# Splitting the row gathers of the value stage into an up half and a down half

## Chip, cores and metric

The kernel runs on one core of one Trainium2 chip. The metric is the device time of one execution in microseconds (us). The core has five engines that run side by side, each with its own program in order: TensorE (PE, with its weight loads PEld), VectorE (DVE), ScalarE (ACT), GpSimd (POOL) and SyncE (SP). They wait for each other through semaphores. 16 DMA engines move the data; SP, ACT and POOL issue transfers to them, each on a queue of its own.

## What is computed

One layer of a decoder trunk, 512 tokens of width 2048, all in float32: attention and a gated unit, then a product-key expert layer (PEER), then a gate. The change touches the expert layer alone:

```python
N_EXPERTS, PEER_HEADS, PEER_TOPK = 128 * 128, 8, 16

def peer(a, w_q, k1, k2, u_exp, v_exp):
    # experts, gates: for each token and head the 16 best of 16384, and their weights
    ...
    u_sel = jnp.take(u_exp, e_c, axis=0)              # rows of the first matrix
    h = jnp.einsum('bthkd,btd->bthk', u_sel, a_c)     # one dot product per pick
    w = (g_c * jax.nn.gelu(h)).astype(a_c.dtype)
    v_sel = jnp.take(v_exp, e_c, axis=0)              # rows of the second matrix
    return jnp.einsum('bthk,bthkd->btd', w, v_sel)    # weighted sum of the rows
```

Each expert is a row of 2048 numbers (8 KB) in each of the two matrices. A token has 8 x 16 = 128 picks.

## The kernel before, in words

The expert layer is done in two ways. For the first 352 tokens (`TD`) it is dense: all 16384 experts are multiplied through TensorE and gated by a table in device memory that is zero where a token did not pick an expert. For the other 160 tokens (128 in the last tile, 32 more spread as 4 sets over the partitions) rows are gathered, one expert for each of 128 partitions at a time: a **pick**. There are 160 picks (`PICKS`), 0 to 127 for the last tile, 128 to 159 for the 32 tokens.

The dense part has two stages. In the **key stage** each step takes 128 experts of the first matrix. In the **value stage** there are 16 groups of 8 **beats**; a beat takes a tile of 1 MB of the second matrix from `s_pv`, and makes 48 matmuls of 352 columns. Float32 is split in two parts for TensorE, so each beat needs from ScalarE the high half of its weights (`wH`, line 603), and from VectorE the low half (`lo`, `wL`, line 1025), which TensorE waits for. `wH` and `wL` have two buffers each; `raw`, the tile as it was loaded, has four in this stage.

The activations of a group are made one group ahead. For each beat SP loads a tile `pre_in` and a tile of gates `gate_in` (lines 415 and 416), POOL multiplies them (`apply_gates`, line 566), ScalarE writes the high half (`actH`, line 859) and VectorE the low half (`weight_lo`, `actL`, line 1555). SP loads the next pair of tiles when the low half two beats back is written.

A pick is done in these steps. POOL gathers 128 rows of `uv_rows`, a table with the two matrices side by side, into a buffer `rows` of 16 KB a partition (`gather`, line 558). VectorE multiplies the first half by the tokens' activations and sums up (`dot`, line 1529). ScalarE puts the sum through gelu and the gate's weight (lines 876 and 880). VectorE adds the second half times that weight to `hT`, or to `b_acc` for the 32 tokens (`add_row`, lines 1538 and 1543), and counts up `pick_done`. That frees the buffer.

The order is written out by hand. `u_step` and `v_step` say which steps of which picks fall into which beat. The first 64 picks (`U_PICKS`) go with the key stage and share three buffers; 60 of them are gathered there while POOL also scatters gates into device memory (line 539). Picks 64 to 159 go with the value stage and take turns in two buffers, `rows3` and `rows4`; `dot` and `add_row` of them lie one or two to a beat over beats 2 to 119. In a beat VectorE does the first of its pick steps, then `lo`, then its other pick steps, then `weight_lo`:

```python
for o in steps[0:1]:
    pick_step(o)
v_low(g, q)
for o in steps[1:]:
    pick_step(o)
v_end(g, q, g % 2, m, 0)
```

POOL does in each beat the multiply of `apply_gates`, and behind it the gathers of that beat; pick j + 2 is gathered behind the add of pick j.

Of the kernel before, what the change touches and what calls it, by code (L numbers as in the profile page):

```python
# [51 lines left out]
U_PICKS, LATE = 64, 4  # L52
# [16 lines left out]
ROW_AT, ROW_USED, ROW_TURN = [], [], []  # L69
# [83 lines left out]
def trunk_layer(nc, a, stream, out, gates_dram, pre_dram):  # L153
# [8 lines left out]
    def at(name, shape, dt, offset):  # L162
        return nc.alloc_sbuf_tensor_at(name, [P] + shape, dt, offset=base + offset)
# [40 lines left out]
    rows = [at(f"rows{i}", [2, D], F, o) for i, o in enumerate((W0, W0 + 16 * KB, W0 + 32 * KB, A0, A0 + 16 * KB))]  # L204
# [70 lines left out]
    with ctx:  # L275
        ps = ctx.enter_context(nc.psum_tensor("ps", [P, 8, 512], F))

        def sem(name):
            return ctx.enter_context(nc.semaphore(name))
# [41 lines left out]
        gain_row_loaded, tok_done_h, tok_copied, a_tok_ready = (  # L321
            sem("gain_row_loaded"), sem("tok_done_h"), sem("tok_copied"), sem("a_tok_ready"))
        row_landed = [sem(f"row_landed{i}") for i in range(5)]
        dot_done, dot_gelu, pick_weighed, pick_done = sem("dot_done"), sem("dot_gelu"), sem("pick_weighed"), sem("pick_done")
        b_loaded, rep_ready, b_tok_done, b_tok_early, b_tok_ready = (
            sem("b_loaded"), sem("rep_ready"), sem("b_tok_done"), sem("b_tok_early"), sem("b_tok_ready"))
# [146 lines left out]
        def _(pool):  # L473
# [75 lines left out]
            def gather(j):  # L549

                if j == U_PICKS:
                    pool.wait_ge(b_tok_ready, 1)
                if j == A_PICKS:
                    pool.wait_ge(b_loaded, 32 * SETS)
                if ROW_USED[j] >= 0:
                    pool.wait_ge(pick_done, ROW_USED[j] + 1)
                ids = idx_s[:, j:j + 1] if j < A_PICKS else idx_b[:, j - A_PICKS:j - A_PICKS + 1]
                pool.indirect_dma_start(  # L558
                    out=rows[ROW_AT[j]][:, :, :].rearrange("p a d -> p (a d)"), out_offset=None, in_=a["uv_rows"],
                    in_offset=bass.IndirectOffsetOnAxis(ap=ids, axis=0)).then_inc(row_landed[ROW_AT[j]], 16)  # L560
# [7 lines left out]
            for j in range(U_PICKS - LATE + 1):  # L568
                gather(j)
                if j >= 1:  # L570
                    for n in range(added, min(added + 4, HEADS * NTD * TOPK)):
                        add_gates(n)
                        added = n + 1
            assert added == HEADS * NTD * TOPK
            for c in range(GROUP):
                apply_gates(c, c % 2)
                if c % 2 == 0 and U_PICKS - LATE + 1 + c // 2 < U_PICKS:
                    gather(U_PICKS - LATE + 1 + c // 2)
            for j in range(U_PICKS, U_PICKS + 2):
                gather(j)  # L580
# [432 lines left out]
        def _(dve):  # L1013
# [517 lines left out]
            def add_row(j):  # L1531

                dve.wait_ge(pick_weighed, j + 1)
                if j >= 1:
                    dve.wait_ge(pick_done, j)
                v3 = rows[ROW_AT[j]][:, 1, :].rearrange("p (a b) -> p a b", a=KD)
                if j < A_PICKS:
                    V.scalar_tensor_tensor(hT[:, :, TA:T], v3, pick_w[:, j:j + 1], hT[:, :, TA:T],  # L1538
                                           ALU.mult, ALU.add).then_inc(pick_done, 1)
                elif j == A_PICKS:  # L1540
                    V.tensor_scalar(b_acc[:, :, :], v3, pick_wb[:, 0:1], None, ALU.mult).then_inc(pick_done, 1)
                else:
                    V.scalar_tensor_tensor(b_acc[:, :, :], v3, pick_wb[:, j - A_PICKS:j - A_PICKS + 1], b_acc[:, :, :],  # L1543
                                           ALU.mult, ALU.add).then_inc(pick_done, 1)

            def pick_step(o):

                if o % 2 == 0:
                    dot(o // 2)
                else:  # L1550
                    add_row(o // 2)
# [640 lines left out]
```

## Time and profile before

| | |
|---|---|
| median of 3 runs | 3055.32 us (3047.83 to 3064.97) |
| profiled execution, its own time | 3049.59 us |
| its span (first to last instruction) | 3047.9 us |
| TensorE busy (matmuls) | 2972.5 us, 98% of the span |
| VectorE busy | 2208.6 us, 72% |
| ScalarE busy | 1252.3 us, 41% |
| POOL busy | 1223.3 us, 40% |
| moved by the DMA engines | 798.00 MB, 262 GB/s on average |

Shares are means over the whole program, in which the stages have different limits. The value stage runs from about 1782 to 2829 us of the span, the gathers from 1064 to 2742 us. Matmuls are pipelined: one is listed with 0.32 us while the next starts 0.16 us behind it. A line such as "PE ps L1720 <- DVE wL L1025: 36.0, 30, 2.9" reads: TensorE stood idle before the matmul of line 1720, until VectorE had written `wL` in line 1025, for 36.0 us in all, 30 times, at most 2.9 us.

### The profile page before, as it was taken

The numbers are of one execution on the slowest core, as the hardware profiler recorded it, in microseconds if no ns is written. First come the engines' busy times: TensorE is split into PE (matmuls) and PEld (weight loads), VectorE is DVE, ScalarE is ACT, GpSimd is POOL, SyncE is SP. The second block draws the span as 40 slices with busy tenths as digits, with TensorE's granted clock in tenths as the row PEclk, the third lists the DMA queues.
The fourth block names the chain that finished last, engine by engine and source line by source line (L and its number), as shares of the span: only waits on it lengthen the run. The fifth ranks groups of instructions, "written<-read, shape, count | busy, mean of one in ns | idle before, by whom it ended". The sixth has DMA issues, their size and how long they took to land.

```text
span 3047.9 us, 43192 instructions
## 1 busy us (share of the span) xinstructions
PE 2972.5 (98%) x16888; PEld 2784.3 (91%) x16888; DVE 2208.6 (72%) x2801; ACT 1252.3 (41%) x1818; POOL 1223.3 (40%) x717
## 2 busy tenths in 40 slices
PE   9999999999999999999999999999999999999998
PEld 7888678899999999999999999999999999999887
DVE  5466754579788777777777678878877888886545
ACT  5224542333332433333333334555555545555422
POOL 1010000018888888888887123233323244540000
PEclk9999999999999999999999999999999999999999
DMA  8462222235545599999999799999999999994222
GB/s 294 164 238 83 70 97 96 83 125 137 133 127 139 131 379 339 360 356 359 357 344 372 299 359 370 397 376 389 393 396 384 383 374 385 370 360 164 97 96 97
DMA packets 191348, 798.00 MB, mean 262 GB/s; under 512 B 66672, under 2 KB 119936, under 8 KB 127200
## 3 DMA queue, kind: packets, MB, share of 16 engines
q1 hardware_dynamic: 90768, 405.36, 36.3%
q0 software_dynamic: 81616, 367.62, 33.2%
q10 hardware_dynamic: 18816, 23.11, 2.2%
q8 instruction: 85, 1.39, 0.2%
q14 instruction: 63, 0.52, 0.0%
HBM read 745.46 MB, written 50.51 MB: 261 GB/s over the span
## 4 chain that ended last, share of the span: by engine, by line
PE 33%; POOL 24%; DMA 21%; DVE 12%; issue 7%; ACT 2%; SPq 0%; ACTq 0%; DVEq 0%; POOLq 0%
POOL gates L539 22%; PE ps L1720 10%; PE ps L1721 10%; PE ps L1722 10%; DMA rows<-uv_rows,idx_s 9%; DMA gate_in<-gates 6%; DMA rows<-uv_rows,idx_b 4%; DVE wL L1025 4%; DVE rows L1529 2%; DVE hT L1538 2%; POOL rows L558 2%; DMA gates<-gates_r,idx_d 1%; DVE b_acc L1543 1%; POOL pre_in L566 1%; ACT wH L603 1%
## 5 line engine op out<-in xcount | busy, mean ns | idle before, releaser
L1720 PE MATMUL ps<-aH,wH 128*128 128x352 f32 (+2 forms) x3088 | 1063.0, 344 | 8.1 <-DVE wL L1025 8.1
L1721 PE MATMUL ps<-aL,wH 128*128 128x352 f32 (+2 forms) x3088 | 1059.3, 343 | 0.0
L1722 PE MATMUL ps<-aH,wL 128*128 128x352 f32 (+2 forms) x3088 | 1059.0, 343 | 0.0
L1025 DVE TENSOR_TENSOR wL<-raw,wH 128x2048 fp32r<-128x2048 f32 x333 | 778.7, 2338 | 195.6 <-ACT wH L603 194.4
L539 POOL DMA_INDIRECT gates<-gates_r,idx_d x384 | 754.1, 1964 | 381.8 <-DVE gates_r L1440 244.5
L603 ACT ACTIVATE wH<-raw 128x2048 fp32r<-128x2048 f32 x333 | 636.5, 1911 | 657.4 <-PE ps L1722 630.3
L1720 PE MATMUL ps<-actH,wH 128*128 128x352 f32 x2048 | 669.1, 327 | 37.0 <-DVE wL L1025 36.8
L1721 PE MATMUL ps<-actL,wH 128*128 128x352 f32 x2048 | 665.4, 325 | 0.0
L1722 PE MATMUL ps<-actH,wL 128*128 128x352 f32 x2048 | 665.0, 325 | 0.0
L1720 PEld LDWEIGHTS ps<-aH,wH 128*128 128x128 f32 x3088 | 581.0, 188 | 49.9 <-DVE wL L1025 8.4
L1721 PEld LDWEIGHTS ps<-aL,wH 128*128 128x128 f32 x3088 | 581.0, 188 | 38.4 <-issue 0.7
L1722 PEld LDWEIGHTS ps<-aH,wL 128*128 128x128 f32 x3088 | 581.0, 188 | 38.3
L1720 PEld LDWEIGHTS ps<-actH,wH 128*128 128x128 f32 x2048 | 388.5, 190 | 47.1 <-DVE wL L1025 46.8
L1722 PEld LDWEIGHTS ps<-actH,wL 128*128 128x128 f32 x2048 | 388.9, 190 | 0.0
L1721 PEld LDWEIGHTS ps<-actL,wH 128*128 128x128 f32 x2048 | 388.8, 190 | 0.0
L1529 DVE SCALAR_TENSOR_TENSOR rows<-rows,ps 128x2048 f32<-128x2048 f32 x128 | 292.2, 2283 | 122.8 <-DMA rows<-uv_rows,idx_s 122.4
L566 POOL TENSOR_TENSOR pre_in<-pre_in,gate_in 128x352 f32<-128x352 f32 x128 | 183.2, 1432 | 336.0 <-DMA gate_in<-gates 335.5
L558 POOL DMA_INDIRECT rows<-uv_rows,idx_s x128 | 188.2, 1470 | 321.2 <-DVE hT L1538 287.9
L1538 DVE SCALAR_TENSOR_TENSOR hT<-rows,pick_w,hT 128x2048 f32<-128x2048 f32 x128 | 301.4, 2355 | 0.6 <-ACT pick_w L880 0.5
L1449 DVE TENSOR_TENSOR ut<-ps,rstd 128x352 f32<-128x352 f32 x128 | 67.0, 524 | 148.1 <-PE ps L1722 139.9
L876 ACT ACTIVATE dots<-dots 128x1 f32<-128x1 f32 x128 | 26.0, 203 | 358.9 <-DVE rows L1529 356.6
L1555 DVE TENSOR_TENSOR actL<-pre_in,actH 128x352 fp32r<-128x352 f32 x128 | 74.9, 585 | 50.0 <-ACT actH L859 50.0
(270 smaller groups left out, 2251.2 us busy)
## 6 DMA issues: line engine op xcount, KB each, us to landing
raw<-s_pu SPq DMA_DIRECT2D x128, 1024.0 KB
raw<-s_pv SPq DMA_DIRECT2D x128, 1024.0 KB, 7.1
gates<-zeros POOLq DMA_DIRECT2D x22, 1024.0 KB, 8.5
pre<-ut ACTq DMA_DIRECT2D x128, 176.0 KB
pre_in<-pre SPq DMA_DIRECT2D x128, 176.0 KB, 7.6
gate_in<-gates SPq DMA_DIRECT2D x128, 176.0 KB, 8.9
raw<-s_out SPq DMA_DIRECT2D x16, 1024.0 KB
raw<-s_pq SPq DMA_DIRECT2D x16, 1024.0 KB
```

The costliest lines, as they stand in the source:

```text
L539: pool.indirect_dma_start(out=gates_flat, out_offset=bass.IndirectOffsetOnAxis(ap=idx_d[0:m, t, c:c + 1], axis=0), in_=gates_r[0:m, t, c:c ...
L558: pool.indirect_dma_start(out=rows[ROW_AT[j]][:, :, :].rearrange("p a d -> p (a d)"), out_offset=None, in_=a["uv_rows"], in_offset=bass.In ...
L566: nc.gpsimd.tensor_tensor(pre_in[b][:, :], pre_in[b][:, :], gate_in[b][:, :], ALU.mult).then_inc(act_gated, 1)
L603: A(wH[parity][:, :], raw[at_n][:, :], ACT.Copy).then_inc(hi_ready, 1)
L1025: V.tensor_tensor(wL[parity][:, :], src[:, :], wH[parity][:, :].bitcast(F), ALU.subtract).then_inc(lo_ready, 1)
L1449: V.tensor_tensor(ut[b][:, :], ps[:, 6 + b, 0:TD], rstd[:, 0:TD], ALU.mult).then_inc(chunk_scaled, 1)
L1529: V.scalar_tensor_tensor(r3, r3, 1.0, act_of, ALU.mult, ALU.mult, accum_out=d).then_inc(dot_done, 1)
L1538: V.scalar_tensor_tensor(hT[:, :, TA:T], v3, pick_w[:, j:j + 1], hT[:, :, TA:T], ALU.mult, ALU.add).then_inc(pick_done, 1)
L1555: V.tensor_tensor(actL[b][:, j, 0:TD], src[:, :], actH[b][:, j, 0:TD].bitcast(F), ALU.subtract).then_inc(act_wlo, 1)
L1720: mm(out, wh, xh, start=start, stop=False, skip_group_check=skip_group_check)
L1721: mm(out, wh, xl, start=False, stop=False, skip_group_check=skip_group_check)
L1722: return mm(out, wl, xh, start=False, stop=stop, skip_group_check=skip_group_check)
```

## The change

For picks 64 to 159 `gather` issues two indirect DMAs instead of one: the first brings 128 rows of 8 KB of the first matrix into the first half of the buffer, the second the rows of the second matrix into the other half. They come from two new tables, `u_rows` and `v_rows`; `uv_rows` stays for picks 0 to 63. The first half counts up the semaphore that the joint row had, the second one of two new semaphores, for which `add_row` waits. `dot` waits as before.

```diff
+        v_row_landed = [sem(f"v_row_landed{i}") for i in range(2)]
...
                 ids = idx_s[:, j:j + 1] if j < A_PICKS else idx_b[:, j - A_PICKS:j - A_PICKS + 1]
+                if j >= U_PICKS:
+                    for half, landed, table in ((0, row_landed[ROW_AT[j]], a["u_rows"]), (1, v_row_landed[ROW_AT[j] - 3], a["v_rows"])):
+                        pool.indirect_dma_start(
+                            out=rows[ROW_AT[j]][:, half, :], out_offset=None, in_=table,
+                            in_offset=bass.IndirectOffsetOnAxis(ap=ids, axis=0)).then_inc(landed, 16)
+                    return
                 pool.indirect_dma_start(
                     out=rows[ROW_AT[j]][:, :, :].rearrange("p a d -> p (a d)"), out_offset=None, in_=a["uv_rows"],
...
                 dve.wait_ge(pick_weighed, j + 1)
+                if j >= U_PICKS:
+                    dve.wait_ge(v_row_landed[ROW_AT[j] - 3], 16 * ROW_TURN[j])
...
+        "u_rows": v["peer_u"][0],
+        "v_rows": v["peer_v"][0],
```

On POOL, at the first beats of the value stage that gather, the program before has this order; `rows_89` and `rows_90` are the two buffers, and the words in brackets are the semaphores that a row waits for:

```order
L558 DMA rows_89<-uv_rows,idx_s 128x4096 [waits pick_done]
L566 TENSOR_TENSOR pre_in_134<-pre_in_134,gate_in_136 128x352 [waits gates_loaded0,pre_loaded0]
L558 DMA rows_90<-uv_rows,idx_s 128x4096 [waits pick_done]
L566 TENSOR_TENSOR pre_in_135<-pre_in_135,gate_in_137 128x352 [waits gates_loaded1,pre_loaded1]
L558 DMA rows_89<-uv_rows,idx_s 128x4096 [waits pick_done]
```

The same place with the change (its lines lie some lower, so 566 is 573):

```order
L561 DMA rows_89<-u_rows,idx_s 128x2048 [waits pick_done]
L561 DMA rows_89<-v_rows,idx_s 128x2048
L573 TENSOR_TENSOR pre_in_134<-pre_in_134,gate_in_136 128x352 [waits gates_loaded0,pre_loaded0]
L561 DMA rows_90<-u_rows,idx_s 128x2048 [waits pick_done]
L561 DMA rows_90<-v_rows,idx_s 128x2048
L573 TENSOR_TENSOR pre_in_135<-pre_in_135,gate_in_137 128x352 [waits gates_loaded1,pre_loaded1]
L561 DMA rows_89<-u_rows,idx_s 128x2048 [waits pick_done]
L561 DMA rows_89<-v_rows,idx_s 128x2048
```

Nothing changed its place; a second gather without a wait of its own stands between each gather and the multiply behind it.

On VectorE, in the middle of the value stage, with the change:

```order
L1547 SCALAR_TENSOR_TENSOR hT<-rows_89,pick_w,hT 128x16x128 [waits pick_done,v_row_landed0,pick_weighed]
L1032 TENSOR_TENSOR wL_73<-raw_69,wH_71 128x2048 [waits hi_ready]
L1536 SCALAR_TENSOR_TENSOR rows_90,dots<-rows_90,ps 128x2048 [waits row_landed4]
L1564 TENSOR_TENSOR actL_85<-pre_in_135,actH_83 128x352 [waits act_whi]
L1547 SCALAR_TENSOR_TENSOR hT<-rows_90,pick_w,hT 128x16x128 [waits pick_done,v_row_landed1,pick_weighed]
L1032 TENSOR_TENSOR wL_74<-raw_70,wH_72 128x2048 [waits hi_ready]
```

The instructions and their order are those of before (lines 1538, 1025, 1529 and 1555 there); only the waits for `v_row_landed` are new, and a `lo` stands behind each such add.

## Rows read from the trace of the kernel before

**Rows 1.** Windows: busy time, matmuls (x), mean clock, DMA share; key stage twice, value stage.
```profile
core 0: us, PE busy (x) PEld busy (x) DVE busy (x) ACT busy (x) POOL busy (x), PEclk, DMA share, GB/s
1150.00:1350.00 200.00, 200.00 (x1252) 200.00 (x1251) 155.46 (x110) 69.52 (x91) 168.88 (x94) 1.00 0.99 350
1350.00:1550.00 200.00, 198.74 (x1243) 198.45 (x1242) 155.87 (x109) 68.00 (x91) 165.58 (x94) 1.00 1.01 357
...
1782.50:2829.40 1046.90, 1009.91 (x6194) 999.63 (x6192) 835.98 (x593) 543.51 (x923) 346.00 (x216) 0.99 0.92 363
```
**Rows 2.** Waits from 1790 to 2735 us: total us, times, longest.
```profile
DVE rows L1529 <- DMA rows<-uv_rows,idx_s: 96.6, 45, 4.5
...
PEld ps L1720 <- DVE wL L1025: 45.7, 33, 3.2
...
PE ps L1720 <- DVE wL L1025: 36.0, 30, 2.9
DVE rows L1529 <- DMA rows<-uv_rows,idx_b: 35.3, 18, 3.4
```
**Rows 3.** Timeline of VectorE: start, duration, instruction, idle time before it and releaser.
```profile
2340.01 2.29 DVE L1529 SCALAR_TENSOR_TENSOR rows<-rows,ps 128x2048 f32<-128x2048 f32 x1 [3.18 <-DMA rows<-uv_rows,idx_s]
...
2343.29 0.53 DVE L1555 TENSOR_TENSOR actL<-pre_in,actH 128x352 fp32r<-128x352 f32 x1 [0.99 <-ACT actH L859]
2343.73 2.35 DVE L1538 SCALAR_TENSOR_TENSOR hT<-rows,pick_w,hT 128x2048 f32<-128x2048 f32 x1
2345.99 2.28 DVE L1025 TENSOR_TENSOR wL<-raw,wH 128x2048 fp32r<-128x2048 f32 x1
...
2360.36 2.29 DVE L1529 SCALAR_TENSOR_TENSOR rows<-rows,ps 128x2048 f32<-128x2048 f32 x1 [4.54 <-DMA rows<-uv_rows,idx_s]
...
2362.57 2.28 DVE L1025 TENSOR_TENSOR wL<-raw,wH 128x2048 fp32r<-128x2048 f32 x1
```
**Rows 4.** Timeline of TensorE, the matmul behind the first of these chains.
```profile
2348.33 0.42 PE L1720 MATMUL ps<-actH,wH 128*128 128x352 f32 x1 [1.63 <-DVE wL L1025]
```
**Rows 5.** Windows of 3.5 us, behind a long stall and behind a short one.
```profile
2003.50:2007.00 3.50, 3.50 (x16) 3.50 (x15) 3.30 (x3) 2.83 (x6) 1.31 (x2) 0.56 0.88 274
...
2349.00:2352.50 3.50, 3.50 (x24) 3.50 (x23) 3.50 (x3) 2.62 (x7) 1.09 (x2) 1.00 0.90 299
```
**Rows 6.** The gathers of line 558 from 1780 to 2760 us.
```profile
DMA to landing us min/median/max: 9.8/11.7/15.8
```
**Rows 7.** Chain of waits from 1790 to 2735 us, shares by line.
```profile
by line: DMA rows<-uv_rows,idx_s 27.9%; DMA gate_in<-gates 17.9%; DMA rows<-uv_rows,idx_b 12.2%; DVE wL L1025 9.1%; DVE rows L1529 7.3%; DVE hT L1538 7.1%; issue 7.1%; POOL pre_in L566 3.2%; DVE b_acc L1543 2.9%; DVE actL L1555 1.4%; ACT ac
```
**Rows 8.** Window of the value stage's body.
```profile
1790.00:2735.00 945.00, 908.82 (x5561) 899.01 (x5560) 767.72 (x526) 491.45 (x854) 335.20 (x210) 0.99 0.97 383
```
**Rows 9.** The page's DMA parts: a queue's packets, MB and share; an issue's KB and landing.
```profile
q1 hardware_dynamic: 90768, 405.36, 36.3%
q0 software_dynamic: 81616, 367.62, 33.2%
...
raw<-s_pv SPq DMA_DIRECT2D x128, 1024.0 KB, 7.1
```
**Rows 10.** Timeline of POOL, two gathers one behind the other.
```profile
1063.64 1.01 POOL L558 DMA_INDIRECT rows<-uv_rows,idx_s  x1 [0.30 <-issue]
1064.95 0.98 POOL L558 DMA_INDIRECT rows<-uv_rows,idx_s  x1 [0.30 <-issue]
```
**Rows 11.** Timeline of POOL, a gather beside the `lo` of 2345.99.
```profile
2346.35 2.78 POOL L558 DMA_INDIRECT rows<-uv_rows,idx_s  x1 [4.63 <-DVE hT L1538]
```
**Rows 12.** Multiplies of line 566 from 1790 to 2735 us, and waits there.
```profile
L566 POOL TENSOR_TENSOR pre_in<-pre_in,gate_in x117: 942/956/3059, 1789.9 to 2728.3; 128x352 f32<-128x352 f32 x117
...
POOL pre_in L566 <- DMA gate_in<-gates: 315.1, 103, 8.8
...
DVE actL L1555 <- ACT actH L859: 42.8, 38, 4.0
```
**Rows 13.** Timelines of VectorE and POOL: a `lo` behind a multiply that was still waiting.
```profile
2441.79 3.03 DVE L1025 TENSOR_TENSOR wL<-raw,wH 128x2048 fp32r<-128x2048 f32 x1
...
2440.38 2.29 POOL L566 TENSOR_TENSOR pre_in<-pre_in,gate_in 128x352 f32<-128x352 f32 x1 [0.90 <-DMA gate_in<-gates]
```

## Prediction, before the change was run

> **What bounds the kernel now.** I read the windows by stage first, then the waits of the value stage, then single beats. In the key stage, while the same kind of gathers runs, TensorE is busy for 200.00 us of 200 and then for 198.74 of 200 [rows 1]. In the value stage the first and the last matmul lie 1046.9 us apart, for 128 beats of 48 matmuls (6144), so 8.18 us a beat. The key stage made 1252 matmuls in 200 us, which is 7.67 us for 48. At that pace the value stage would take 982 us, so about 65 us of it is lost; 50 of the 6194 matmuls in that window are not the beats' own and take some 8 us, which leaves 57 us.
>
> The waits say what is late [rows 2]: TensorE stands for 36.0 us (30 times) before a matmul, its weight load for 45.7 us (33 times), both for VectorE's low half of the weights, `lo`. VectorE itself stands for a gathered row, 96.6 and 35.3 us, 63 times. Single beats join the two. In one, the dot of a pick waits 3.18 us for its row, then come the low half of an activation, the add of the pick and `lo`, and TensorE gets its weights 1.63 us late, at 2348.33 [rows 3, 4]. In the other shape the dot waits 4.54 us and `lo` follows it at once. Of the stalls from 1850 to 2735 that are longer than half a microsecond there are 25, and all have such a dot less than 10 us ahead, 12 in the first shape, 13 in the second. A long stall costs more than itself: behind the stall at 2003, a stretch of 3.5 us has a mean clock of 0.56 where a beat with a short stall has 1.00 [rows 5]. That is the lower of the two levels, 1.2 GHz instead of 2.4, for nearly all of it. Five such stretches stand in this stage's body (from 1874, 2003, 2522, 2587 and 2720), so some 5 x 1.7 = 8.5 us.
>
> So the bound of this stage is a loop through two row buffers: pick j is added, POOL gathers pick j+2 into the same buffer, the row lands 11.7 us (median; 9.8 to 15.8) behind its issue [rows 6], the dot may start. TensorE pays for its late turns. The chain of waits of this stage says the same: 27.9 and 12.2% of it are rows on their way, 17.9% the gates' tiles [rows 7].
>
> **What the change does, step by step.** It touches picks 64 to 159 alone, the ones of the value stage.
>
> 1. *The dot waits for half the bytes.* The first half should land sooner by what the other half took on the queue. At the stage's 383 GB/s [rows 8] the 1 MB that no longer lies ahead is 2.7 us. The nearest row for a transfer of 1 MB is that of the weights, 7.1 us to landing [rows 9], and 11.7 - 7.1 = 4.6 us. Nothing at all is the lower bound, if the engines' queues are so full that order decides. I take 2.7, the careful end of the two measured prices. The row waits are 131.9 / 63 = 2.1 us each and at most 4.5, so with 2.7 us most are gone.
>
> 2. *The add has a new wait.* The second half is issued behind the first. Two gathers one behind the other took POOL 1.01 and 0.98 us with 0.30 us between them [rows 10]; but a gather issued while a `lo` runs on VectorE takes 2.78 us [rows 3, 11]. So the second half is issued 1.3 to 3.1 us later than the joint row was, and lands at 11.7 + 1.3 = 13.0 to 14.8 us. (The Trainium skill, SBUF — State Buffer, Who interferes with whom, infers that a tensor_tensor does not hold up descriptor generation. By that only the 1.3 would stand. The trace has 2.78 us beside a `lo`, which is one, so it speaks against it.) The dot starts at 9.0 and ends at 11.3. In the first shape the add started 3.7 us behind the dot's start [rows 3], which would be 12.7. So there the second half is the later by 0.3 to 2.1 us, and the chain is 0.6 to 2.4 us earlier than before (15.4), not 2.7. In the second shape nothing stands between dot and `lo`, so it gains all 2.7. Of the mean of the two views of the stall, (36.0 + 45.7) / 2 = 41 us, I keep 5 us for the first shape: 36 us go. With them go the low clocks, 8 us. Gross: 44 us.
>
> 3. *The loop still closes.* From issue to landing of the second half at most 14.8 us, add 2.35 us: 17.2 us, and the buffer has 2 x 945 / 93 = 20 us between its turns (93 picks in 945 us). This is why I don't expect the new wait to become the bound.
>
> 4. *POOL issues 96 gathers more*, 1.3 to 3.1 us each, 125 to 298 us. It was busy for 346 of 1046.9 us [rows 1], so there is room in sum. Behind each pair stands a gating multiply, of which the body of the stage has 117; they waited for their own data 315.1 us in 103 turns, 3.1 us each [rows 12]. That wait hides one more gather, whether it meets `lo` or not. The other 14 have no such cover: 14 x 1.3 = 18 us at least come later. Behind them wait ScalarE's high half and VectorE's low half of the activations, which are used by TensorE a whole group of eight beats later; they reach TensorE only where VectorE stands for them ahead of the next `lo`. It stood for them 42.8 us in 38 turns, mostly the 0.98 us in which ScalarE first weighs the pick [rows 3, 12]. I price this at 3 us, with 0 and 18 as ends.
>
> 5. *The transfers.* Bytes are the same, packets are smaller. SP's queue, mostly packets of 8 KB, moved 405.36 MB in 36.3% of the engines' time; POOL's queue, mostly 16 KB rows, 367.62 MB in 33.2% [rows 9]. Per MB that is equal within 1%. So splitting costs nothing on the engines themselves. But they have little left: 0.97 busy over the body of this stage [rows 8], and 0.99 and 1.01 in the two stretches of the key stage in which TensorE was hardly stopped [rows 1]. If all of the stage's transfers must be squeezed into less time, the share rises with it. From 0.97 to 0.99 that allows 2.0% of 945 us, 19 us; to 1.01, 4.0%, 37 us. The middle is 28 us, less than the 44 of step 2, so **this is the end that I take**.
>
> The Trainium skill has two rules on this (DMA: Bandwidth & Descriptors). Its section Measured and the one on the anatomy of a DMA give about 2.0 us fixed for each DMA plus bytes / 436 GB/s: by that the first half lands 2.4 us sooner, and step 2 would keep some 1 us per stall more. Its section Where 436 GB/s comes from names some 358 GB/s as what HBM gives a core when both cores of a pair stream and 435 as the fabric's ceiling. The trace has 383 GB/s with this core alone, so the lower figure doesn't bind here; by the higher one some 13% would be left, and step 5 would cap nothing.
>
> 6. *The waits themselves:* VectorE gets 96 semaphore waits more on instructions that it issues anyway, with 945 - 768 = 177 us idle in this stretch [rows 8]; nothing.
>
> **The sum.** 28 us by the transfers' limit, less 3 us of POOL: 25 us. Against the profiled execution (3049.59 us, span 3047.9) that gives 3024.6. The median of the runs shown is 5.7 us above that execution, so for the median I say 3055.3 - 25 = 3030 us. A difference of 0.5%, 15 us, is about what a measurement of this kernel can tell from none.
>
> **Rivals.**
> - *The DMA engines are full already* (0.97 is their end; the queues' order only decides who waits). Then the half that comes early is paid by the other half, by the gates or by the next row: in the first shape the add stands where the dot stood, and the chain to `lo` ends when it did. For it: bits of idle in the engines come only when both row buffers are taken. Against it: 1.01 in the key stage. Gain 0 to 14 us, 3041 to 3055. Here belongs the case in which the change doesn't do what it says, because the first half of pick j+2 queues behind the second half of pick j+1. By the rule of 358 GB/s this would be the outcome too; that sentence changes no number. Chance 0.30.
> - *POOL becomes late* (the other sign). A pair of gathers holds POOL up to 5.8 us where both meet a `lo`. The multiply behind it then starts while VectorE is in a long instruction, and the next `lo` is stretched: 3.03 us with a multiply that was still waiting, against 2.28 [rows 3, 13]. If each of the 96 further gathers pushes a multiply into this, it costs 96 x 0.75 = 72 us of VectorE. VectorE has a fifth of its time free, so I count half, 36 us, on the way to TensorE; with the 18 us of step 4 that is 54 us against the 28 gained: 26 us slower, 3081. It decides from the point where the multiplies without a wait for their data are a majority. Against it: POOL's wait of 3.1 us on average. Milder forms end at 3071. Chance 0.14.
> - *The forecast's own spread*: all 44 us go (3011) or 16 only (3039). Chance 0.56.
>
> So: faster by over 0.5% 0.56, within it 0.30, slower 0.14. The range reaches from 3002 (all of the 57 us of the stage's loss but a few) to 3062, which takes in the no-change case with the spread of its runs (3047.83 to 3064.97) and leaves most of the slower one out.
>
> **What would show it.** Waits of the dot for rows well under half of 131.9 us; a new wait of the add for the second table, a few tens of us; TensorE's wait for `lo` below 15 us and fewer low clocks; the body at a DMA share of 0.99 or more, over 390 GB/s; POOL's gathers 96 more at 1.0 or 2.8 us, its wait for the gates' data smaller. I am wrong if the dot's wait shrinks and TensorE's doesn't (then the add or the gates took its place), if the share stays at 0.97 with the same pace, or if `lo` at 3.0 us becomes common.

## The result, and the profile after

The changed kernel takes 3004.12 us (median, 3000.28 to 3008.28), the kernel before, measured beside it, 3051.57 us (3045.14 to 3064.97): 47 us less, ratio 0.985 (95% interval 0.9823 to 0.9878). A second measurement gave 2999.9 us against 3053.32, ratio 0.9829 (0.9814 to 0.9844). The forecast had the sign and the mechanism, and only half of the size: 25 us, with 3030 as the time. Its range, 3002 to 3062, just takes in the first of the two medians and not the second. One of the six executions of e8b below took 7626.78 us at a mean TensorE clock of 0.488; it counts in that run's median (3001.35 without it) and not in its ratio.

The windows of the profile after, in the columns of [rows 1]:

```profile
1150.00:1350.00 200.00, 196.24 (x1219) 195.07 (x1218) 153.97 (x108) 67.84 (x90) 168.98 (x90) 1.00 0.99 341
1350.00:1550.00 200.00, 194.98 (x1208) 193.53 (x1207) 150.15 (x106) 66.47 (x86) 165.06 (x93) 1.00 0.99 348
...
1790.00:2690.00 900.00, 895.88 (x5579) 893.35 (x5578) 783.01 (x528) 495.58 (x854) 485.60 (x303) 1.00 1.00 402
```

The last row answers to [rows 8]: TensorE is busy for 896 of 900 us, the mean clock is 1.00 where it was 0.99, and the DMA engines move 402 GB/s instead of 383. From its first to its last matmul the value stage takes 996.9 us:

```profile
1790.30:2787.20 996.90, 992.78 (x6195) 990.15 (x6193) 852.19 (x593) 546.11 (x923) 506.64 (x312) 1.00 0.95 382
```

It was 1046.9 [rows 1], so 50 us went there, more than the span lost in all (3047.9 to 3006.1, 42 us). The difference lies in the key stage: in this execution the value stage begins 8 us later. Its program is the one of before; a later section comes back to it.

The waits from 1790 to 2690 us after, columns as in [rows 2]:

```profile
POOL pre_in L573 <- DMA gate_in<-gates: 234.8, 80, 9.1
ACT actH L866 <- POOL pre_in L573: 135.7, 67, 6.0
...
DVE actL L1564 <- ACT actH L866: 75.1, 59, 6.5
...
DVE rows L1536 <- DMA rows<-u_rows,idx_b: 12.6, 12, 2.8
DVE rows L1536 <- DMA rows<-u_rows,idx_s: 10.2, 18, 1.4
PEld ps L1729 <- DVE wL L1032: 6.7, 9, 1.5
PE ps L1729 <- DVE wL L1032: 3.9, 6, 1.2
...
DVE b_acc L1552 <- DMA rows<-v_rows,idx_b: 0.9, 1, 0.9
```

The dot's wait for its row fell from 131.9 us [rows 2] to 22.8. TensorE's wait for `lo` fell from 36.0 to 3.9 us, that of the weight load from 45.7 to 6.7. The new wait, of the add for the second table, came up once, for 0.9 us. What grew stands behind POOL: ScalarE waited 135.7 us for the gating multiply, and VectorE 75.1 us for ScalarE's half, 42.8 before [rows 12]. In the kernel before, from 1790 to 2735 us, the first of these two was:

```profile
ACT actH L859 <- POOL pre_in L566: 18.8, 21, 5.6
```

What the two cost TensorE can be no more than its few us of waits that are left.

The landings of the two gathers, from the page's view of the DMA issues (median from issue to landing):

```profile
raw<-s_pv SPq DMA_DIRECT2D x128, 1024.0 KB, 9.2
...
rows<-u_rows,idx_s POOLq DMA_INDIRECT x64, 9.1
rows<-v_rows,idx_s POOLq DMA_INDIRECT x64, 10.6
```

The joint row took 11.7 us [rows 6], the first half now takes 9.1: 2.6 us sooner. The second half takes 10.6 from its own issue, which lies 1.3 us behind the first one where nothing holds it up. The weights' tile lands at 9.2 instead of 7.1 us [rows 9]; it has slack, ScalarE waited for it once, for 0.9 us.

### The profile page after: what moved, and what is told of

It is laid out like the page before. It is cut to its first block and busy times, and to the rows that moved or that the text cites. A ratio compares the mean times of both kernels' runs of the same rounds, so it can differ in the third digit from the quotient of the medians.

```text
span 3006.1 us, 43288 instructions
## 1 busy us (share of the span) xinstructions
PE 2958.6 (98%) x16888; PEld 2775.7 (92%) x16888; DVE 2226.4 (74%) x2801; ACT 1254.9 (42%) x1818; POOL 1390.1 (46%) x813
## 5 line engine op out<-in xcount | busy, mean ns | idle before, releaser
L1729 PE MATMUL ps<-aH,wH 128*128 128x352 f32 (+2 forms) x3088 | 1063.5, 344 | 12.8 <-DVE wL L1032 12.7
L540 POOL DMA_INDIRECT gates<-gates_r,idx_d x384 | 766.0, 1995 | 384.3 <-DVE gates_r L1447 244.6
L1729 PE MATMUL ps<-actH,wH 128*128 128x352 f32 x2048 | 661.7, 323 | 4.1 <-DVE wL L1032 3.9
L573 POOL TENSOR_TENSOR pre_in<-pre_in,gate_in 128x352 f32<-128x352 f32 x128 | 235.3, 1839 | 251.7 <-DMA gate_in<-gates 250.3
L1536 DVE SCALAR_TENSOR_TENSOR rows<-rows,ps 128x2048 f32<-128x2048 f32 x128 | 292.1, 2282 | 61.3 <-DMA rows<-uv_rows,idx_s 50.7
L1547 DVE SCALAR_TENSOR_TENSOR hT<-rows,pick_w,hT 128x2048 f32<-128x2048 f32 x128 | 320.9, 2507 | 1.2 <-ACT pick_w L887 1.0
L561 POOL DMA_INDIRECT rows<-u_rows,idx_s x64 | 105.3, 1645 | 116.3 <-DVE hT L1547 99.0
```

What stands on the lines that cost most here:

```text
L540: pool.indirect_dma_start(out=gates_flat, out_offset=bass.IndirectOffsetOnAxis(ap=idx_d[0:m, t, c:c + 1], axis=0), in_=gates_r[0:m, t, c:c ...
L561: pool.indirect_dma_start(out=rows[ROW_AT[j]][:, half, :], out_offset=None, in_=table, in_offset=bass.IndirectOffsetOnAxis(ap=ids, axis=0) ...
L573: nc.gpsimd.tensor_tensor(pre_in[b][:, :], pre_in[b][:, :], gate_in[b][:, :], ALU.mult).then_inc(act_gated, 1)
L1536: V.scalar_tensor_tensor(r3, r3, 1.0, act_of, ALU.mult, ALU.mult, accum_out=d).then_inc(dot_done, 1)
L1729: mm(out, wh, xh, start=start, stop=False, skip_group_check=skip_group_check)
```

## The experiments

Theory A was that the time came from the dot's earlier start. The rivals: B, that it was the smaller packets and how they share the engines with SP's queue; C, that the DMA engines, as in my step 5, set the end; D, that POOL sets it. Each ratio is to the kernel before, measured beside the run.

**e1: the dot waits for both halves.** Packets, tables and the further gathers stay.

```diff
                 dve.wait_ge(row_landed[ROW_AT[j]], 16 * ROW_TURN[j])
+                if j >= U_PICKS:
+                    dve.wait_ge(v_row_landed[ROW_AT[j] - 3], 16 * ROW_TURN[j])
```

Expected:

> The change with one wait more: the dot of picks 64 to 159 waits for the second half too. Packets, tables, POOL's 96 further gathers stay. Theory A (the gain is the dot's earlier start): the gain goes, and a little more since the second half is issued 1.3 to 3.1 us later than the joint row was: 3045 to 3080 us, VectorE waits for the second table 130 us or more, TensorE for the low half of the weights 36 us or more. Rival B (the gain is the packets of 8 KB, which share the engines more evenly with SP's queue): 3000 to 3015 us, few waits.

Measured: 3079.6 us, ratio 1.007 (1.0047 to 1.0093) to the kernel before, which was at 3052.96 here. Its waits from 1790 to 2690 us:

```profile
DVE rows L1538 <- DMA rows<-v_rows,idx_s: 106.8, 43, 5.9
...
PEld ps L1731 <- DVE wL L1032: 62.0, 38, 5.1
...
PE ps L1731 <- DVE wL L1032: 50.9, 32, 4.8
DVE actL L1566 <- ACT actH L866: 42.3, 36, 6.5
DVE rows L1538 <- DMA rows<-v_rows,idx_b: 37.5, 12, 5.9
```

The row waits are back, at 144 us and up to 5.9 us long. The whole gain is gone, and 27 us more. Behind a pair's first issue the second half lands 12.6 us later (median over this trace's pairs), where the joint row took 11.7: somebody now waits for the later of two. B falls as the source of the gain, since the packets of 8 KB are all there.

**e2: the second matrix's rows first.**

```diff
-                    for half, landed, table in ((0, row_landed[ROW_AT[j]], a["u_rows"]), (1, v_row_landed[ROW_AT[j] - 3], a["v_rows"])):
+                    for half, landed, table in ((1, v_row_landed[ROW_AT[j] - 3], a["v_rows"]), (0, row_landed[ROW_AT[j]], a["u_rows"])):
```

Expected:

> The change with the two gathers of a pick in the other order, the second matrix's rows first; the dot waits for the gather issued last. Theory A: like e1_dot_waits_both, 3045 to 3080 us. Rival B: 3000 to 3015 us.

Measured: 3076.96 us, ratio 1.0069 (1.0049 to 1.0089). So the order in which a pair is issued decides between 1.5% faster and 0.7% slower. Semaphores, tables and the number of instructions are the same in both.

**e4: no rows of the second matrix.** 94 of the second gathers are left out, and the add takes what lies in the buffer.

```diff
+                        if half == 1 and j >= U_PICKS + 2:
+                            continue
...
-                    dve.wait_ge(v_row_landed[ROW_AT[j] - 3], 16 * ROW_TURN[j])
+                    dve.wait_ge(v_row_landed[ROW_AT[j] - 3], 16)
```

Expected:

> The change without the second matrix's rows for picks 66 to 159: 94 gathers of 1 MB, a quarter of the value stage's bytes, are left out, and the add takes what lies in the buffer. Theory A (after the change the DMA engines are full but TensorE isn't kept from work by them): 2995 to 3005 us, within 10 us of the change, DMA share near 0.78. Rival C (the DMA engines at a share of 1.00 hold the stage back now): the rest of TensorE's waits in the value stage goes, 2985 us or less.

Measured: 2997.28 us, ratio 0.9815 (0.9794 to 0.9835). The windows of its value stage:

```profile
1777.00:2766.60 989.60, 989.07 (x6194) 988.15 (x6192) 822.92 (x593) 544.12 (x923) 341.65 (x218) 1.00 0.79 285
```

With a quarter of the bytes and all of POOL's further gathers away, the stage takes 989.6 us instead of 996.9, with TensorE busy for 989.07 of them. So some 7 us is what transfers, POOL and late rows together cost the changed kernel in this stage (one execution each; in the change's second profile the stage took 999.4 us). C falls for the changed kernel: its share of 1.00 is not what holds it.

**e5: one more tile a beat**, into memory that this stage doesn't use.

```diff
                 sp.dma_start(gate_in[b][:, :], gates_rows[:, c, :]).then_inc(gates_loaded[b], 16)
+                if isinstance(c, int) and c >= 2 * GROUP:
+                    for _ in range(1):
+                        if extra_count[b]:
+                            sp.wait_ge(extra_landed[b], 16 * extra_count[b])
+                        sp.dma_start(ut[b][:, :], pre_dram[c, :, :]).then_inc(extra_landed[b], 16)
+                        extra_count[b] += 1
```

Expected:

> The change plus one further load of 176 KB from the stored tiles into unused memory in each of 112 beats of the value stage: 5.6% more bytes there, which nobody computes with. Rival C, my step 5 (a DMA share of 1.01 is the end): the body would need 1.055 and is stretched by 4% or more: 3040 us or more. Theory A (the share does not show the end, packets of 0.309 us for 8 KB leave room up to 424 GB/s, the body is at 402): little, 3004 to 3020 us.

Measured: 3031.88 us, ratio 0.9948 (0.9932 to 0.9964): between the two, so neither expectation held. The window of its body:

```profile
1790.00:2690.00 900.00, 875.70 (x5415) 869.92 (x5414) 758.36 (x513) 481.59 (x832) 461.72 (x297) 1.00 1.02 413
```

5.6% more bytes made the rate rise to 413 GB/s, not to the 424 that would have kept the pace. The edge is near, but beyond what the change needs. SP's queue didn't wait for the further loads in this window, so it is not the edit's own wait that delays the rest.

**e9: a wider one**, 10% more bytes; the same edit with another source and a target of 640 columns.

```diff
+    extra_in = [at(f"extra_in{i}", [640], F, C0 + 7 * KB + 2560 * i) for i in range(2)]
...
+                        sp.dma_start(extra_in[b][:, :], stream["pv"][c, :, 0:640]).then_inc(extra_landed[b], 16)
```

Expected:

> e5_one_more_tile with a wider load, 320 KB instead of 176 KB, so 10% more bytes in 112 beats. If 413 GB/s is the engines' end, as that run suggests: a beat moves 402 GB/s x 7.79 us = 3.13 MB with the change, 3.46 MB here, 8.37 us at 413 GB/s; times 112 beats, 0.58 us more each: 65 us over the change, 3065 to 3075 us, GB/s near 413. If the stage is held by how late each row is and not by the bytes: the rate rises beyond 413 and the time stays below 3050 us.

Measured: 3078.33 us, ratio 1.008 (1.0063 to 1.0096), 78 us above the change's second measurement (2999.9), beside which it ran.

```profile
1790.00:2690.00 900.00, 851.36 (x5166) 842.64 (x5165) 724.79 (x491) 458.63 (x794) 433.42 (x282) 0.98 1.02 410
```

More demand gave no more rate: 410 GB/s after 413. The time is 3 us above the 3065 to 3075 that 413 gave; with the measured 410 in the same sum a beat takes 3.46 MB / 410 GB/s = 8.44 us, which is 73 us. So the mean rate of this stage's mixture ends at 410 to 413 GB/s, with a share of 1.02. Single slices of 22.5 us reach 419 in e5 and 421 in e9, and 424 already in the body of the kernel before, beside others of 349: its own profile had stretches well above its mean.

**e6: POOL gets three small memsets behind each pair.**

```diff
+                    for i in range(3 if j >= U_PICKS + 2 else 0):
+                        if j > U_PICKS + 2 or i:
+                            pool.wait_ge(filled, 3 * (j - U_PICKS - 2) + i)
+                        nc.gpsimd.memset(ut[0][:, :], 0.0).then_inc(filled, 1)
```

Expected:

> The change plus three small memsets on POOL behind each pair of gathers of picks 66 to 159, as a dearer pair would be (some 1 us a pick, read from its trace). If POOL has the room that its 46% of busy time says: 3000 to 3010 us. If POOL is near its end, since ScalarE now waits for its multiply 135.7 us where it was 18.8: 3015 us or more, with stretched instructions of VectorE.

Measured: 3002.09 us, ratio 0.9848 (0.9823 to 0.9873). POOL is busy for 573 of 900 us instead of 486, and the time stays:

```profile
1790.00:2690.00 900.00, 896.76 (x5579) 894.13 (x5578) 785.62 (x530) 496.50 (x860) 572.99 (x580) 1.00 1.00 402
```

**e7: all 160 picks split**, those of the key stage too.

```diff
-                if j >= U_PICKS:
-                    for half, landed, table in ((0, row_landed[ROW_AT[j]], a["u_rows"]), (1, v_row_landed[ROW_AT[j] - 3], a["v_rows"])):
+                if True:
+                    for half, landed, table in ((0, row_landed[ROW_AT[j]], a["u_rows"]), (1, v_row_landed[ROW_AT[j]], a["v_rows"])):
...
-                if j >= U_PICKS:
-                    dve.wait_ge(v_row_landed[ROW_AT[j] - 3], 16 * ROW_TURN[j])
+                dve.wait_ge(v_row_landed[ROW_AT[j]], 16 * ROW_TURN[j])
```

Expected:

> The change for all 160 picks, the 64 of the key stage too. There POOL is busy 84% of the time with scattering gates, and gets 64 gathers more of 1.3 us: 83 us. Theory A: row waits of the key stage (25 to 50 us, of which TensorE feels 5 to 10) go, but POOL's later gates may be waited for: 2995 to 3015 us. Rival D (POOL is the bound of the key stage): the scatter ends some 80 us later and the value stage's first gates are late: 3030 us or more.

Measured: 3103.82 us, ratio 1.0179 (1.0154 to 1.0204), about 100 us above the change. One window of its key stage, its waits from 1060 to 1780 us, and POOL's timeline there:

```profile
1150.00:1350.00 200.00, 177.73 (x1052) 175.61 (x1051) 134.05 (x95) 58.84 (x78) 170.24 (x98) 0.96 0.92 307
```

```profile
DVE rows L1536 <- DMA rows<-u_rows,idx_s: 118.0, 37, 6.6
PEld ps L1728 <- DVE wL L1032: 74.2, 23, 6.1
PE ps L1728 <- DVE wL L1032: 67.5, 23, 5.8
```

```profile
1202.88 1.55 POOL L540 DMA_INDIRECT gates<-gates_r,idx_d  x1 [0.30 <-issue]
1204.74 1.36 POOL L561 DMA_INDIRECT rows<-u_rows,idx_s  x1 [0.30 <-issue]
1206.40 1.87 POOL L561 DMA_INDIRECT rows<-v_rows,idx_s  x1 [0.30 <-issue]
1208.58 1.61 POOL L540 DMA_INDIRECT gates<-gates_r,idx_d  x1 [0.30 <-issue]
```

Here POOL hardly ever waits for data: every instruction shown starts 0.30 us behind the last one, 170 of 200 us are busy, and 98 times 0.30 us is the rest. It was as full before (168.88 us busy with 94 instructions [rows 1]), so each further gather delays all that stands behind it. From 1060 to 1780 us the dots wait for rows 118 us, where they waited 25.9 in the kernel before and 50.7 in the change's first profile, and TensorE pays 67.5 us and runs at a mean clock of 0.96 in the window shown. The last scatter of gates ends at 1754.5 us instead of 1666.5, as D had it, but the loss is taken in the key stage itself: the value stage begins at 1878.1 us (1790.5 in the change) and then takes 1001.1 us. D is right for the key stage: the split that gains 1.5% in one stage loses more than twice that in the other.

**e8: the first half already behind the dot.** Pick j+2's first half is gathered when the dot of pick j is done, its second half behind the add as now.

```diff
-                if ROW_USED[j] >= 0:
+                if halves == (0,):
+                    pool.wait_ge(dot_done, ROW_USED[j] + 1)
+                elif ROW_USED[j] >= 0:
                     pool.wait_ge(pick_done, ROW_USED[j] + 1)
...
-                        if o % 2 == 1 and o // 2 + 2 < PICKS:
-                            gather(o // 2 + 2)
+                        if o // 2 + 2 < PICKS:
+                            gather(o // 2 + 2, (o % 2,))
```

Expected:

> The change, with the first half of pick j+2 gathered as soon as the dot of pick j is done, a step before its add; the second half behind the add as now. Theory A: the row waits left in the value stage (23 us) go, but TensorE waits only some 5 us there: 2998 to 3006 us, no difference to the change. Rival C: the engines are full and the earlier half delays the second half and the gates: 3005 to 3020 us.

Measured: 3001.02 us, ratio 0.9814 (0.9791 to 0.9836). The wait for the first half is practically gone (from 22.8 us to 0.8), TensorE's is 2.4 us:

```profile
PE ps L1733 <- DVE wL L1036: 2.4, 3, 1.6
...
DVE rows L1540 <- DMA rows<-u_rows,idx_s: 0.6, 3, 0.2
DVE rows L1540 <- DMA rows<-u_rows,idx_b: 0.2, 1, 0.2
```

**a1 and e8b: the change and this version again**, measured side by side.

> The change itself once more, beside e8b_up_half_after_dot on the same chip: 3000 to 3008 us. Its key stage, whose program is that of before, should wait for rows as before (some 25 us) if the 50 us in the first profile of the change were chance.

> The kernel of e8_up_half_after_dot once more, to settle whether it beats the change. Theory A: TensorE lost only 5 us in the value stage to waits with the change and 3 us in this one, so the two are within 0.15%, 4 us, and the intervals overlap. If the earlier half is worth more than the profile shows: 2995 us or less with the change at 3004.

Measured: 2999.9 us, ratio 0.9829 (0.9814 to 0.9844), and 3002.22 us, ratio 0.983 (0.9812 to 0.9847). No difference. What the earlier half removes is a wait that TensorE no longer felt. In a1 the key stage had few waits:

```profile
DVE rows L1536 <- DMA rows<-uv_rows,idx_s: 9.6, 6, 3.9
...
PE ps L1729 <- DVE wL L1032: 1.3, 1, 1.3
```

Those are its waits from 1060 to 1700 us. In the change's first profile the same two were 50.0 us and 8.7 us, in that of before 24.6 and 4.1. Across the profiled executions of all programs with this key stage, the dots' waits there range from 6.8 us (e8) to 50.0 and TensorE's from nothing to 8.7 (e8b had 20.4 and none). In the other runs that have the new tables and this key stage the value stage begins between 1777.0 and 1787.0 us, in the kernel before at 1782.5, in the change's first profile at 1790.5. So the 8 us by which it began late there vary from execution to execution and are no effect of the new tables. The variation's source was not looked for.

## Why the prediction was wrong in its size

**Step 1, the dot's lead: right.** I took 2.7 us and a landing at 9.0 us; measured were 2.6 and 9.1. The row waits fell to a sixth. The 2.4 us that I had worked out by the Trainium skill (DMA: Bandwidth & Descriptors, Anatomy of one DMA) lies as near, but the "some 1 us per stall more" that I drew from it doesn't follow: 2.4 us is 0.3 less than 2.7.

**Step 2, the add's wait: priced too dear.** I kept 5 us of stalls for it; the wait occurred once, for 0.9 us. The second half needs 10.6 us from its issue, not the 11.7 that I gave it. From the issue of the first half it landed 12.4 us later in the median of the 96 pairs, and 16.0 at most, where I had 13.0 to 14.8; that even the late ones were hardly waited for says that most adds lie later than the 12.7 us of the one chain I had read. The gross of 44 us was 36 of waits and 8 of low clock. TensorE's waits fell by 32 us in one view and 39 in the other. Its low clocks are gone too: the value stage before had six, the sixth at 2782 us, behind the body that I had counted, for some 20 us in all at the lower level, which is 10 us of work; the change's first profile has none. That makes 42 to 49 us; the stage got shorter by 50.

**Step 3, the loop closes: right** (that one wait of 0.9 us).

**Step 4, POOL: small as priced, though its side effects came.** The 3 us weren't measured by themselves; e4 puts some 7 us as the most for POOL, transfers and late rows together, and with the 87 us of POOL work that e6 added the time stayed. POOL's busy time in the stage rose from 346 to 507 us: 129 us are the further gathers, at the low end of the 125 to 298 of step 4, another 52 us are longer multiplies, and the first gathers took 19 us less than the joint ones. Here is what the second rival feared, first POOL's timeline, then VectorE's:

```profile
2320.48 2.77 POOL L561 DMA_INDIRECT rows<-u_rows,idx_s  x1 [2.93 <-DVE hT L1547]
2323.55 0.95 POOL L561 DMA_INDIRECT rows<-v_rows,idx_s  x1 [0.30 <-issue]
2326.03 0.95 POOL L573 TENSOR_TENSOR pre_in<-pre_in,gate_in 128x352 f32<-128x352 f32 x1 [1.53 <-DMA gate_in<-gates]
```

```profile
2320.13 2.28 DVE L1032 TENSOR_TENSOR wL<-raw,wH 128x2048 fp32r<-128x2048 f32 x1
...
2326.04 3.08 DVE L1547 SCALAR_TENSOR_TENSOR hT<-rows,pick_w,hT 128x2048 f32<-128x2048 f32 x1
2329.05 2.28 DVE L1032 TENSOR_TENSOR wL<-raw,wH 128x2048 fp32r<-128x2048 f32 x1
```

The add that starts while a multiply runs on POOL takes 3.08 us. Of the 96 adds of the value stage 42 take 3.0 us or more, 2 did before, and at the start of each of them a multiply had 0.9 us still to run. 42 x 0.7 = 29 us of VectorE, where the rival had counted 96 x 0.75 = 72 and put half of that on TensorE's way. VectorE had lost its row waits, and this filled the place: it was idle for 117 of 900 us and still in time. e6 shows that POOL's own room isn't used up either.

**Step 5, the transfers: this is the step that failed.** I read the end of the DMA engines off the share, 0.99 to 1.01 in a stage without stalls, and set the limit at 19 to 37 us, the middle of 28 in place of the 44. Two things were wrong in it. The key stage has its share of 1.0 at 350 to 357 GB/s, with POOL scattering gates there, one number at a time: from 1150 to 1550 us before, 20628 packets of 4 bytes took 8% of the engines' time for 0.08 MB. A share at one mixture says nothing on the bytes that another can move. And the rate doesn't rise in proportion to the share, so a share of 1.0 is not the end: the body went from 0.97 to 1.00 while its rate rose by 402 / 383 = 5%, and the stage got 50 us shorter where my conversion gives 28 for a share of 1.00. The packets of the body show where the rest came from. Those of 8 KB on SP's queue took 379 ns in the mean at 297 GB/s (e4), 341 at 384 (before), 326 at 402 (the change) and 317 at 413 (e5): in these runs each packet was shorter the more was moved, so a high share still held time that more bytes could use. Why that is so no run shows. It isn't the size of the rows: e1 has the change's packets, and at its 373 GB/s those of SP's queue took 348 ns.

e5 and e9 measure the end: 410 to 413 GB/s at a share of 1.02. Against 383 GB/s that is a limit of 7 to 8%, 62 us or more of 945, above the 50 that TensorE had to give, so the limit doesn't cut the sum at all. Without it the prediction's own sum is 44 less 3: 41 us, for a median of 3014; the interval around the measured 47 us (0.9823 to 0.9878 of 3051.57 is 37 to 54 us) holds that.

The Trainium skill (DMA: Bandwidth & Descriptors, Where 436 GB/s comes from) gives 435 GB/s as the fabric's ceiling. By that nothing would have been capped, as it came out; the measured end is 94 to 95% of it. The other figure there, 358 GB/s from HBM, which it says binds for transfers between HBM and SBUF, was passed in the value stage's body by every run here but e4, which leaves bytes out (before 384, after 402). The same page of the Trainium skill, in its section Measured, ties 358 GB/s to two cores that stream, and no run here had a second one.

**The rivals.** The first, full engines, held for the kernel with 5.6% more bytes, not for this one. The second, POOL late, is the key stage's truth (e7), not the value stage's: the majority of multiplies there (80 of 116, 103 of 117 before) still wait for their data, and only from the point where they no longer do had I let it decide.

## What to carry to other kernels

A gather whose parts are used at different times can be split for the first user, if the issuing engine has idle time and the first part is issued first; the other order, or a first user that waits for both, is worse than no split. Before a limit is read from the DMA share, look at the GB/s in single slices of the same stage (424 at best before), or add a known load and see whether the rate follows. A waiting time may be large and cost little: what counted was whether `lo` came in time.

## What the runs showed of the hardware

- Splitting rows from 16 to 8 KB cost next to nothing on the engines. From 1790 to 2690 us POOL's queue (`q0`) took 38.7 us of engine time for a MB before and 38.9 after, SP's (`q1`) 42.3 and 40.9. The shares of 16 engines are, first before, then after:

```profile
q0 software_dynamic: 12848, 187.18, 50.3%
q1 hardware_dynamic: 48174, 157.98, 46.4%
```

```profile
q0 software_dynamic: 26784, 195.05, 52.7%
q1 hardware_dynamic: 50678, 165.84, 47.1%
```

- The DMA share alone is no measure of room: SP's packets of 8 KB shortened from 379 to 317 ns as the rate rose from 297 to 413 GB/s.
- An add of VectorE that started while a POOL multiply on SBUF was still running was stretched from 2.34 to some 3.05 us, 42 times.
- The gathers in POOL's queue took 0.95 or some 2.8 us. In the last tile's picks all 23 long ones began beside a `lo` (above, 2320.48 beside 2320.13), and a pair's second gather began beside none: its median was 0.949 us. In the 32 tokens' picks it was long too, with a median of 2.31 us (`idx_b` below), beside their dots and adds:

```profile
L561 POOL DMA_INDIRECT rows<-v_rows,idx_s x64: 937/949/1262, 1797.0 to 2401.0; - x64
L561 POOL DMA_INDIRECT rows<-v_rows,idx_b x32: 945/2310/2913, 2408.0 to 2705.4; - x32
```

- Whether rows in two tables of their own differ from halves out of the joint table wasn't tried. The two tables alone don't bring the gain: e2 has them and loses all of it.
